# Joint products in the third down stage, its low halves added by GpSimd, and modulation products of the last up stages laid over it

## What is computed, cut to what matters

```python
h = x + jnp.concatenate([gla_out, nsa_out], axis=-1) @ w_out
m = rms_norm(h, ffn_norm_g)
return h + (jax.nn.silu(m @ w_gate) * (m @ w_up)) @ w_down      # 5632 hidden features
```

```python
shift, scale, gate = _modulation(c, mod_w, mod_b)               # silu(c) @ mod_w + mod_b, 3 x 2048
h  = _rmsnorm(x, pre_g) * (1 + scale) + shift
hc = _rmsnorm(ctx, pre_g) * (1 + scale_c) + shift_c
```

## Time and profile before

| what | value |
|---|---|
| median of 3 runs | 2010.0 us (2009.75 to 2010.97) |
| the profiled execution | 2010.92 us |
| its span | 2009.3 us |
| up2 and up2b | about 1013 to 1153 us of the span |
| down2 | about 1153 to 1227 us |
| TensorE, VectorE, ScalarE, GpSimd busy | 98%, 80%, 48%, 11% of the span |

### The profile page before, as it was taken

The page is one execution under the profiler, slowest core; times in us unless marked ns, Lnnn a source line. Parts: engine busy times, 40 slices in busy tenths (PEclk is TensorE's granted clock), DMA queues, the critical chain, the costliest instruction groups (busy, mean ns, idle before and its releaser), DMA issues.

```text
span 2009.3 us, 35456 instructions
## 1 busy us (share of the span) xinstructions
PE 1971.5 (98%) x12894; PEld 1783.0 (89%) x12894; DVE 1606.1 (80%) x2193; ACT 964.6 (48%) x1443; POOL 211.8 (11%) x294
## 2 busy tenths in 40 slices
PE   7999999999999999999999999999999998999997
PEld 7998898899888888888888899887889988999986
DVE  6996677757888998889999878779986777678754
ACT  6543446645444344444444454236464455554453
POOL 0000000011000220001311111111000131000011
PEclk9999999999999999999999999999999999999998
DMA  7554554356777787777888874677656884568563
GB/s 238 168 163 132 168 189 127 106 166 199 232 230 232 266 316 233 237 237 244 286 287 299 297 263 166 212 240 225 206 179 219 264 283 157 192 196 291 189 189 126
DMA packets 121150, 434.46 MB, mean 216 GB/s; under 512 B 13248, under 2 KB 15680, under 8 KB 120784
## 3 DMA queue, kind: packets, MB, share of 16 engines
q1 hardware_dynamic: 92240, 328.11, 49.7%
q0 software_dynamic: 28800, 104.87, 15.9%
HBM read 430.83 MB, written 2.10 MB: 215 GB/s over the span
## 4 chain that ended last, share of the span: by engine, by line
PE 84%; DVE 9%; DMA 4%; issue 2%; ACT 1%; SPq 0%; DVEq 0%; POOL 0%; POOLq 0%; ACTq 0%
PE ps L647 29%; PE ps L648 15%; PE ps L634 9%; PE ps L635 9%; PE ps L636 8%; DVE w_lo L1683 3%; DMA side<-w_side 3%; PE ps L782 2%; PE ps L1096 1%; PE ps L1106 1%; PE ps L715 1%; PE ps L717 1%; PE ps L716 1%; DVE mod_sum L1700 1%; PE ps L824 1%
## 5 line engine op out<-in xcount | busy, mean ns | idle before, releaser
L647 PE MATMUL ps<-ba_act,w_hi 128*128 128x512 f32 x3008 | 1062.5, 398 | 3.9 <-DVE w_lo L1683 3.7
L648 PE MATMUL ps<-ba_act,w_lo 128*128 128x256 f32 x3008 | 841.6, 280 | 0.0
L1683 DVE TENSOR_TENSOR w_lo<-raw,w_hi 128x1024 fp32r<-128x1024 f32 x610 | 728.7, 1236 | 35.1 <-ACT w_hi L1260 34.3
L1260 ACT ACTIVATE w_hi<-raw 128x1024 fp32r<-128x1024 f32 x610 | 612.6, 1042 | 224.6 <-PE ps L636 158.9
L647 PEld LDWEIGHTS ps<-ba_act,w_hi 128*128 128x128 f32 x3008 | 565.2, 188 | 138.9 <-issue 4.5
L648 PEld LDWEIGHTS ps<-ba_act,w_lo 128*128 128x128 f32 x3008 | 568.0, 189 | 1.3 <-issue 1.2
L634 PE MATMUL ps<-ba_act,w_hi 128*128 128x256 f32 x1168 | 335.3, 287 | 5.8 <-DVE w_lo L1683 5.3
L636 PE MATMUL ps<-ba_act,w_lo 128*128 128x256 f32 x1168 | 331.7, 284 | 0.0
L635 PE MATMUL ps<-ba_act,w_hi 128*128 128x256 f32 x1168 | 331.6, 284 | 0.0
L1700 DVE SCALAR_TENSOR_TENSOR mod_sum<-side,csil,mod_sum 128x1024 f32<-128x1024 f32 x180 | 228.6, 1284 | 37.6 <-DMA side<-w_side 34.8
L542 POOL DMA_DIRECT2D side<-w_side x200 | 107.7, 538 | 1356.8 <-DVE mod_sum L1700 773.5
(11 more groups left out here) (364 smaller groups left out, 1852.8 us busy)
## 6 DMA issues: line engine op xcount, KB each, us to landing
raw<-w_main SPq DMA_DIRECT2D x610, 512.0 KB, 4.4
side<-w_side POOLq DMA_DIRECT2D x200, 512.0 KB, 4.6
x_tok<-x_in SPq DMA_DIRECT2D x4, 512.0 KB, 7.6
ctx_tok<-ctx_tok SPq DMA_DIRECT2D x1, 2048.0 KB, 11.3
y_out<-res SPq DMA_DIRECT2D x4, 384.0 KB, 3.1
table<-counts_tab SPq DMA_DIRECT2D x1, 512.0 KB, 13.9
y_out<-res SPq DMA_DIRECT2D x2, 256.0 KB, 3.0
cons<-cons_in SPq DMA_DIRECT2D x1, 478.0 KB, 10.4
```

The costliest lines, as they stand in the source:

```text
L647: pe.matmul(ps[:, bank, :], wh, act[:, kt, :, :], start=first and b == 0, stop=False)
L648: mm = pe.matmul(ps[:, bank, 0:T], wl, act[:, kt, 0, :], start=False, stop=last and b == 7)
L1260: act.activation(w_hi[:, slot, 0:n], raw[:, slot, 0:n], ACT.Copy).then_inc(hi_ready, 1)
L1683: dve.tensor_tensor(w_lo[:, slot, 0:n], raw[:, slot, 0:n], w_hi[:, slot, 0:n].bitcast(F32), ALU.subtract)\
```

## The change

down2 becomes a joint stage with low halves added by GpSimd, a step's square one step behind; the blocks of a step are 8 and 4, so `joint_products` gets their number. Eight of the 32 modulation strips of up2 and up2b go to down2, one in each even step; up2 now makes 12 strips, up2b the last 4 of up2 and 8 of its own. The sum of up2 goes to step 4 of up2b, the sum of up2b to step 14 of down2, there with products by a column of ones into bank 7. The gate of the attention layer (`ev_gate`), which needs this sum, is made in ev_kv.

```diff
 def products(stage, k):
+    if stage == "up2":
+        return [(stage, k)]
+    if stage == "up2b":
+        return [("up2", 12 + k) if k < 4 else (stage, k - 4)]
+    if stage == "down2":
+        return [("up2b", 8 + k // 2)] if k % 2 == 0 else []
...
-JOINT = ("gout", "nkv", "up0", "down0", "up1", "down1", "up2", "up2b", "ev_q", "ev_q2", "ev_out", "od_out")
+JOINT = ("gout", "nkv", "up0", "down0", "up1", "down1", "up2", "up2b", "down2", "ev_q", "ev_q2", "ev_out", "od_out")
-LOW_ADDED = ("down0", "down1")
+LOW_ADDED = ("down0", "down1", "down2")
-MOD_BANK = {"ev_kv": 4, "ev_q": 6, "ev_q2": 6, "ev_out": 7}
+MOD_BANK = {"up2b": 7, "ev_kv": 4, "ev_q": 6, "ev_q2": 6, "ev_out": 7}
-SUMS_STEP = {"ev_q2": 1, "ev_z": 1}
+SUMS_STEP = {"up2b": 4, "down2": 14, "ev_q2": 1, "ev_z": 1}
...
+            def low_add(stage, k):
+                pool.wait_ge(S("low_out"), low_outs(stage, k))
+                pool.wait_ge(dve_read, dve_reads(stage) + k + 1)
+                pool.tensor_tensor(res[:, k, :], res[:, k, :], up_x[:, k % 2, :], ALU.add).then_inc(S("low_added"), 1)
...
-            mod_loads(group_start("up2") + 2, group_start("ev_kv") + 2)
+            m1 = group_start("ev_kv") - 6
+            mod_loads(group_start("up2") + 2, m1)
             for k in range(16):
-                add_square(1, k)
+                if k % 2 == 0:
+                    side_load(0, m1 + k // 2 + 2 * CMP_HALVES, (mods_added, m1 + k // 2 - 1))
+                low_add("down2", k)
+                if k:
+                    add_square(1, k - 1)
+            add_square(1, 15)
...
                 steps(pe, stage, body,
-                      first=COUNT[stage] if chain is not None else 2 if split or stage in SUMS_OF else 0)
+                      first=COUNT[stage] if chain is not None or stage in SUMS_STEP else 2 if split or stage in SUMS_OF else 0)
...
-                run(f"down{c}", (b_hi, b_lo) if last else b_act, kt=n, split=[("gate_lo", silus)],
+                run(f"down{c}", b_act, kt=n, split=[("gate_lo", silus)],
...
                     else:
+                        act.wait_ge(S("low_added"), 32 + k + 1)
                         src = of[:, k:k + 1, :] if isinstance(i, int) else of[:, bass.ds(i * 2 + k, 1), :]
...
-                    ahead(f"down{c}", squared="ev", of=res, chain=ctx_chain())
+                    ahead(f"down{c}", squared="ev", of=res, chain=ctx_chain(), low=lambda k: up_x[:, k % 2, :])
...
-                        for m in products(stage, k):
-                            add_mod(stage, i, m)
+                        for group, m in products(stage, k):
+                            add_mod(group, i, m)
```

More of the change, by code:

```diff
@@ L90, in products @@
 def products(stage, k):
+    if stage == "up2":
[4 more added lines that the diff above has]
+        return [("up2b", 8 + k // 2)] if k % 2 == 0 else []
     if stage not in MOD_GROUPS:
-        return ()
+        return []
     n = COUNT[stage]
     if stage in SECOND:
-        return (k // 2,) if k % 2 else ()
-    return range(DT * k // n, DT * (k + 1) // n)
-JOINT = ("gout", "nkv", "up0", "down0", "up1", "down1", "up2", "up2b", "ev_q", "ev_q2", "ev_out", "od_out")
-LOW_ADDED = ("down0", "down1")
+        return [(stage, k // 2)] if k % 2 else []
+    return [(stage, m) for m in range(DT * k // n, DT * (k + 1) // n)]
+JOINT = ("gout", "nkv", "up0", "down0", "up1", "down1", "up2", "up2b", "down2", "ev_q", "ev_q2", "ev_out", "od_out")
+LOW_ADDED = ("down0", "down1", "down2")
 SUM_LAST = ("ev_out", "od_out")
@@ L603, in loads_and_low @@
                     side_load(0, m0 + k + 2 * CMP_HALVES, (mods_added, m0 + k - 1))
-                    pool.wait_ge(S("low_out"), low_outs(stage, k))
-                    pool.wait_ge(dve_read, dve_reads(stage) + k + 1)
-                    pool.tensor_tensor(res[:, k, :], res[:, k, :], up_x[:, k % 2, :], ALU.add).then_inc(S("low_added"), 1)
+                    low_add(stage, k)
             for k in range(8):
@@ L637, in half_products, with joint_products @@
                 return mm
-            def joint_products(bank, c, par, act, first, last, split=None):
+            def joint_products(bank, c, par, act, first, last, split=None, blocks=8):
                 slot = 2 * par + c
-                for b in range(8):
+                for b in range(blocks):
                     wh, wl = w_hi[:, slot, b * P:(b + 1) * P], w_lo[:, slot, b * P:(b + 1) * P]
@@ L647, in joint_products @@
                     pe.matmul(ps[:, bank, :], wh, act[:, kt, :, :], start=first and b == 0, stop=False)
-                    mm = pe.matmul(ps[:, bank, 0:T], wl, act[:, kt, 0, :], start=False, stop=last and b == 7)
+                    mm = pe.matmul(ps[:, bank, 0:T], wl, act[:, kt, 0, :], start=False, stop=last and b == blocks - 1)
                 return mm
@@ L665, in step @@
                     if stage in JOINT:
-                        mm = joint_products(par, c, par, act, c == 0, c == 1, waits)
+                        mm = joint_products(par, c, par, act, c == 0, c == 1, waits, nb)
                     else:
@@ L2212, in ctx_chain @@
                         then(dve.tensor_scalar(qn_neg[:, :], col("ev_qn"), -1.0, None, ALU.mult))
-                    if t == 2:
-                        dve.wait_ge(S("mods_read"), 6)
-                        dve.tensor_tensor(ev_gate[:, :], mods[:, 32:48, 0], col("ev_post", 0, 16), ALU.mult)
                     if t == 4:
@@ L2322, in ev_chain @@
                     yield
+                    if t == 2:
+                        dve.wait_ge(S("mods_read"), 6)
+                        dve.tensor_tensor(ev_gate[:, :], mods[:, 32:48, 0], col("ev_post", 0, 16), ALU.mult)
                     if t == 3:
```

## The result

The changed kernel takes 2018.98 us (median of 5, 2016.42 to 2020.58), the kernel before in the same rounds 2009.75 (median of 5): **1.0046 times as long, 95% interval 1.0036 to 1.0056**, +9.2 us. It lies within the stated range of 2006.0 to 2019.5 and on the forecast's side, but 3.1 above the forecast of 2015.9 and 1.0 above the 2013 to 2018 that the prediction gave for the forecast alone; what holds it in the range is the room that was left for R3.

A forecast was written before the change was run, and what follows sets the result against it. TensorE, busy 98% of the span, was taken as the bound. Terms -4.0 - 0.6 - 0.8 - 2.6 + 0.8 + 7.0 + 4.9 + 1.2 = +5.9 on 2010.0 gave 2015.9 us, range 2006.0 to 2019.5.

The forecast's parts named there:

- R3: Rival, up2, up2b and down2's first steps: products get no cheaper, 0.353 a block; +8.9, 2018.9 us; chance 0.11.
- a: up2 and up2b: fewer modulation products, so TensorE no longer waits for w_lo; -4.0 us, at most -4.3.
- b: First down2 step: gating of up2b's last tile in time, -0.6 us; up2b's eight sum transposes leave, -0.8.
- c: down2: joint products take 4.16 instead of 4.33 us a step, -2.6 over 16 steps if TensorE sets the pace.
- d: down2: ScalarE and VectorE wait on each other in a ring, one turn a step; ScalarE's low copy lengthens 4.69 to 4.97.
- e: down2: one of GpSimd's two additions a step holds up VectorE's w_lo by 0.54 us, making the ring 5.51.
- f: down2: the ring's cost, one earlier stall of +0.8 us, then seven turns from step 8 to 15, +7.0.
- g: down2 step 14: TensorE waits for up2b's last modulation product and its sum, delaying step 15; +4.9 us.
- h: Norm behind down2: last square waits for the low copy, read and GpSimd's addition; +1.2 us, bounds 0 and 1.8.
- i: Others: moved loads, GpSimd's queue, ev_gate moved to ev_kv, up2b unrolled on TensorE; cost 0.
- R1: Rival, down2: GpSimd's additions do not meet VectorE's w_lo, ring 4.97; +0.6, 2010.6 us; chance 0.20.
- R2: Rival, down2: the ring does not close, TensorE's step stays longest at 4.57; -6.6, 2003.4 us; chance 0.16.

The follow-up runs named there:

- after: The changed kernel with the whole change in, against the kernel before: 2018.98 us, 1.0046 times as long.
- e1: Changed kernel with all 32 modulation products back in up2 and up2b and up2b's sum in down2's first step; joint down2 kept: 2016.92 us, 1.0039 of before.
- e10: The changed kernel run and profiled once more, no edit: 2019.35 us, 1.0049 of the kernel before.
- e5: Changed kernel with ScalarE's context tile one step later and up2b's sum behind step 15: 2005.0 us, 0.9983 of the kernel before.
- e4: Changed kernel with ScalarE rounding each context tile one step later, sum left in step 14: 2011.71 us, 1.0013 of the kernel before.
- e8: Changed kernel with down2 as before (not joint), eight modulation products over it, up2b's sum behind step 15: 2004.36 us, 0.998 of the kernel before.
- e9: Changed kernel without GpSimd's additions of the low half and of the squares in down2: 2011.86 us, 1.0016 of the kernel before.
- e7: Changed kernel without GpSimd's addition of the low half in down2, waits and counts kept: 2013.53 us, 1.0026 of the kernel before.
- e6: Changed kernel with 38 unread 256-column products on TensorE ahead of its wait for the sum in step 14: 2016.38 us, 1.0038 of the kernel before.
- e3: Changed kernel with up2b's sum moved behind step 15 and read in ev_kv: 2015.07 us, 1.003 of the kernel before.
- e2: Changed kernel with down2 as before (not joint), eight modulation products over it, sum in step 14: 2007.56 us, 0.9995 of the kernel before.

## Why the prediction was right, and where it was short

The forecast's own case came true: the turns at 5.5 from step 8, the gap at the sum, pairs of 2.36. It was short by 3.3 (+5.9 for +9.2). By its parts:

- **a** (-4.0): -4.4. The up stages run at 5.545 a step beside three sums, as the bound had it.
- **b** (-0.6 and -0.8): right in kind. No wait for gating in after; in e1, where the second product is back, it is there (1.39).
- **c** (-2.6): 4.16 in the first steps as forecast, though 4.24 in e10, the same kernel. With a context tile in the step the joint form gains 0.07 (e5) to 0.14 (e4) against the 4.75 of e8, not 0.165. Over the stage it is worth about 1.0 (e5 against e8, 0.6 and 0.4 of waits). From step 7 on the ring hides even this.
- **d, e** (ring 5.51): 5.49; without the additions 4.96 for 4.97 (e9). The size of the hold was right, and that one of the two additions hits each pair. But the prediction pointed at the new one, released by the read; in the rows the low half's addition meets every second pair and the square's the others. That is why e7, without the low half's addition, freed every other pair only. The Trainium skill (SBUF — State Buffer, "SBUF: two separate sides") says that of a VectorE operation with two SBUF inputs and a GpSimd operation that reads SBUF, the one that starts first keeps their shared port for its whole instruction. Taken as the 0.74 of GpSimd's row, that gave turns of 5.7; the runs show 5.49, a hold of 0.53. Whether the lock is shorter than GpSimd's row no run shows.
- **f** (+0.8 and +7.0): the ring is the cost of which one edit takes back the most, and its seven turns take 38.4 (1179.68 to 1218.12) for 38.6. Opening it (e4) gives 7.0, of which 2.4 is the shorter wait at the sum and 4.6 the steps.
- **g** (+4.9) **is the term that failed.** The prediction had the product at S + 4.5 and the start of step 15 at S + 6.2, S being the start of w_lo of step 15. S was 1218.12. The product was there at S + 5.1 (1223.24), since the 1.74 was the time of a pair that meets no addition, and part e had just priced the hold at 0.54; I used it in the ring and left it out here. And step 15 started at S + 8.55 (1226.67), because the one-column products ran at 1.2 GHz, 3.43 for 1.70, and then step 15's first blocks did, 1.5 more. The 1.70 had been taken from a place where TensorE had not stood still before (1325.28 in the kernel before, no wait ahead of it). e6, which keeps TensorE busy while it waits, takes 3.1 back. 0.6 + 1.7 + 1.5 = 3.8 are missing in g, and 0.2 in h. Against it stand 0.4 more gain in a and 0.4 to 0.5 less cost than forecast in the rest of down2, which leaves 3.2 in the traces, 3.3 in the medians.
- **h** (+1.2): +1.4. The 1.7 between e5 and e8 holds about 0.75 (3.54 - 2.79) that belongs to the long addition of step 14 in e5.
- **i** (0): one more wait stands here, that of TensorE for the context's last low half. In after it is covered by the wait at the sum; take that away and it is late next: 2.11 in e3, 3.27 in e1.

R1 (the additions do not meet) is what e9 makes by force; its ring of 4.97 was right. R2 (it all fits) needed a ring under 4.57 and lost to 5.49. R3 (blocks of 0.353) did not occur in the profile of after, where the copies of down2's first steps are 4.16 apart. It did there in e10, the same kernel, and in e1, e3, e4 and e9: 4.24 a step is 0.353 a block. That is 0.3 over four steps. The up stages took 130.15 in both profiles, and why a block takes the one or the other no run here shows. R3's time of 2018.9 is next to the result by chance.

Open: whether the halved clock has its cost in after at 3.1 (after against e6) or, as e10 with its longer stretch has it, at 4.4; the runs show both.

## What to carry to other kernels

Where one engine's in-order queue waits for a tile of another, and that one for the first, add up the ring in rows before anything is added to either queue: the busy shares (VectorE 80%, ScalarE 48%) say nothing of it, and moving one consumer a step later may be worth more than the change itself (7.0 us here for one digit). A wait of TensorE of some us is priced with what comes behind it at half clock: take the durations behind it from rows at that clock, and give the wait something else to multiply, or the waiting work a later place. When two changes come as one, time each alone: the products were worth 5 us with their sum moved, and the joint stage they came with lost more than that.

## What the runs showed of the hardware

- The granted clock of TensorE fell from 1.00 to 0.50 (1.2 GHz) behind idle times of 4.76, 4.31, 3.56, 3.27, 2.40 and 2.11 us (after, e7, e9, e1, e4, e3), and did not behind 1.39 (e1, ahead of down2), 1.12 (e2) or the turns' waits (1.09 the longest, at 1225.25 in e1). What TensorE had done ahead of them differed too, a stage without waits in e2, turns with a wait in most of them in after, so these are cases and not a limit. How long it stayed there differed between two profiles of the same kernel, 6.6 and 8.7 us from the sum on, and was 9.4 in e7. The Trainium skill (TensorE: Matmul & The Clock Gate, "Part 1: The HAM clock gate (the "warmup" mystery)") says that the gate follows how busy TensorE has been of late, and that the number of slow products at the start of one kernel varies from run to run. The rows agree with the first, and show the like of the second behind a wait in the middle of a kernel.
- The hold between VectorE's subtraction and GpSimd's addition goes both ways: the pair takes 2.36 for 1.82, and the addition 1.36 for 0.74 (e7), once 2.90 (e5, 1217.65). An addition of GpSimd held up in this way is late for its next one, so taking one of two away lets the other meet VectorE instead.
- Two profiles of the same kernel can differ in the pace of TensorE with no wait and a granted clock of 1.00 in both: two steps of 12 joint blocks each take 8.34 in after (ScalarE's copies at 1150.51 and 1158.85) and 8.50 in e10 (1150.78 and 1159.28).
